# Start of a two-block kernel on one core: the first norm's remainders ahead of its squares, its sums and its spread inside later weight panels, and the layers of the filter network placed later

## The reference, cut to what matters

```python
def rmsnorm(x, g):
    y = x32 * lax.rsqrt(jnp.mean(x32 * x32, axis=-1, keepdims=True) + RMS_EPS)
    return y * g
...
def hyena_filter(L, w1, b1, w2, b2, w3, b3, freq, w_out, decay):
    act = lambda a: jnp.sin(fr * a)
    h = act(feat @ w1 + b1)
    h = act(h @ w2 + b2)
    h = act(h @ w3 + b3)
    h = (h @ w_out).reshape(L, 2, D_MODEL)
    h = h * jnp.exp(-t[:, :, None] * jnp.abs(decay))
...
def hyena_mixer(u, ...):
    z = short_conv(u @ w_in + b_in, conv_w, conv_b)
```

## Time and profile before

| what | value |
|---|---|
| time, median of 3 runs | 2446.01 us (2444.39 to 2450.88) |
| time of the profiled execution | 2445.98 us |
| its span, first to last instruction | 2444.2 us |
| TensorE busy | 97% of the span |
| VectorE, ScalarE, GpSimd busy | 45%, 25%, 27% of the span |
| mean granted clock of TensorE | 0.986 of full speed |

### The profile page before, as it was taken

How to read it: one execution, slowest core, us unless ns; L and a number is a source line. 1 busy time by engine, 2 the same in 40 slices (tenths; PEclk the granted TensorE clock), 3 DMA queues, 4 the chain that set the end, 5 groups by cost and what they waited for, 6 DMA issues and landing times.

```text
span 2444.2 us, 29269 instructions
## 1 busy us (share of the span) xinstructions
PE 2360.0 (97%) x11692; PEld 1899.7 (78%) x11692; DVE 1107.9 (45%) x1131; ACT 604.0 (25%) x672; POOL 657.8 (27%) x378
## 2 busy tenths in 40 slices
PE   7999999799999999999997999999999999999996
PEld 5666773478888888888886888889897877778885
DVE  6765445542662165413366837263543124500533
ACT  4333324422100001002123636262622011111011
POOL 2212211122333333323241121222222233323331
PEclk9999999999999999999998999999999999999998
DMA  4133239512221223112111212020214221112231
GB/s 155 51 122 123 85 134 369 187 43 78 95 86 52 77 80 109 43 43 70 51 61 35 104 36 69 26 77 26 77 34 181 94 78 56 56 43 69 95 121 69
DMA packets 77507, 211.51 MB, mean 87 GB/s; under 512 B 24182, under 2 KB 28088, under 8 KB 77178
## 3 DMA queue, kind: packets, MB, share of 16 engines
q1 hardware_dynamic: 64794, 172.72, 20.7%
q10 hardware_dynamic: 8288, 29.36, 3.1%
q0 software_dynamic: 4352, 8.40, 1.1%
HBM read 165.36 MB, written 40.37 MB: 84 GB/s over the span
## 4 chain that ended last, share of the span: by engine, by line
PE 75%; DVE 3%; ACT 1%; issue 0%; ACTq 0%; DVEq 0%
PE ps L1209 63%; PE ps L539 5%; DVE T L1857 1%; PE ps L1483 1%; PE ps L586 1%; PE ps L605 1%; PE ps L568 1%; PE ps L606 1%; PE ps L607 1%; PE ps L1231 0%; DVE XN L1887 0%; PE ps L1240 0%; DVE X L2181 0%; DVE H L1880 0%; PE ps L505 0%; PE ps L524 0%
## 5 line engine op out<-in xcount | busy, mean ns | idle before, releaser
L1209 PE MATMUL ps<-H,whi 128*128 128x512 f32 x4000 | 1082.3, 392 | 21.9 <-DVE H L1924 11.3
L1209 PEld LDWEIGHTS ps<-H,whi 128*128 128x128 f32 x4000 | 749.9, 188 | 198.5 <-issue 29.6
L1209 PE MATMUL ps<-H,wlo 128*128 128x512 f32 x2000 | 617.7, 390 | 0.0
L1156 POOL CAST whi<-wraw 128x1024 fp32r<-128x1024 f32 x174 | 182.5, 1049 | 1573.0 <-PE ps L1209 844.9
L1158 POOL TENSOR_TENSOR wlo<-wraw,whi 128x1024 fp32r<-128x1024 f32 x178 | 453.6, 2548 | 53.4 <-ACT whi L673 39.5
L1209 PEld LDWEIGHTS ps<-H,wlo 128*128 128x128 f32 x2000 | 376.5, 188 | 79.3
L1209 PE MATMUL ps<-A,whi 128*128 128x512 f32 x1472 | 397.8, 392 | 8.2 <-DVE A L2213 4.9
L1209 PEld LDWEIGHTS ps<-A,whi 128*128 128x128 f32 x1472 | 278.0, 189 | 68.0 <-issue 5.3
L1209 PE MATMUL ps<-A,wlo 128*128 128x512 f32 x736 | 228.1, 391 | 0.0
L1209 PEld LDWEIGHTS ps<-A,wlo 128*128 128x128 f32 x736 | 139.3, 189 | 29.3
L2097 DVE TENSOR_TENSOR T<-ps,T 128x1024 f32<-128x1024 f32 x22 | 26.9, 1224 | 155.7 <-PE ps L1209 155.7
(11 more groups left out here) (337 smaller groups left out, 2310.6 us busy)
## 6 DMA issues: line engine op xcount, KB each, us to landing
wraw<-in_panels SPq DMA_DIRECT2D x181, 512.0 KB, 3.6
mw<-in_modp SPq DMA_DIRECT2D x24, 512.0 KB, 3.5
g<-gsp SPq DMA_DIRECT2D x16, 512.0 KB, 3.7
gr<-g SPq DMA_DIRECT2D x16, 512.0 KB, 9.8
bs<-s SPq DMA_DIRECT2D x16, 512.0 KB, 9.4
YB<-yi POOLq DMA_DIRECT2D x16, 512.0 KB, 8.8
X<-in_xT SPq DMA_DIRECT2D x4, 1024.0 KB, 10.8
s<-sa SPq DMA_DIRECT2D x8, 512.0 KB, 2.7
```

Source lines behind the costliest of these rows:

```text
L1156: nc.gpsimd.tensor_copy(whi[:, s, :, :], wraw[:, s, :, :]).then_inc(hi_made, 1)
L1209: last = mm(p[:, c * step:(c + 1) * step], w[:, ws, k, :], operand(act, a, k, c * step, step), start=(q == 0 and w is whi and a == 0), sto ...
```

## The change

Only orders change, and who splits panel 1. DVE: all eight remainders first, then the remainder of panel 1, then the eight adds. The argument of the filter's first layer is cut in two around them. The arguments of layers 2 and 3 move behind the panel product of zin1 and zin3. ACT: all rounded copies, then the rounding of panel 1, then the squares. PE: zin1 starts ahead of the norm's sums, which come after its sixth k step. The spread comes in the middle of zin2, and mlp1 and mlp2 come one panel later. GpSimd no longer splits panel 1. SyncE issues `vec` ahead of panel 0 and X tiles 0 and 1 apart.

```diff
-PHASES = [("mlp0", 1, 0), ("zin0", 1, 1), ("norm1", 1, 0), ("zin1", 1, 1), ("mlp1", 1, 0), ("zin2", 1, 1),
-          ("mlp2", 1, 0), ("zin3", 1, 1), ("ztap", len(ZTAP), len(ZPANELS)), ...
+PHASES = [("mlp0", 1, 0), ("zin0", 1, 1), ("zin1", 1, 1), ("norm1", 1, 0), ("zin2", 1, 1), ("mlp1", 1, 0),
+          ("zin3", 1, 1), ("mlp2", 1, 0), ("ztap", len(ZTAP), len(ZPANELS)), ...
...
+            sp.dma_start(vec[:, :], d["vec"]).then_inc(vec_in, 16)
             panel(0, 0)
-            sp.dma_start(vec[:, :], d["vec"]).then_inc(vec_in, 16)
-            for k in range(4):
+            for k in range(2):
+                sp.dma_start(X[:, k, :], xv[:, k, :]).then_inc((cx_in, x_in[0])[k], 16)
+            for k in range(1, 4):
                 sp.dma_start(X[:, 2 * k:2 * k + 2, :], xv[:, 2 * k:2 * k + 2, :]).then_inc(x_in[k], 16)
...
+            pool.wait_ge(split_made, 2)
...
             project("zin0", 0, (n1.lo, 0))
             pe.wait_ge(const_in, 16)
+            project("zin1", 0, part=range(KT - 2))
             norm_sums("norm1", (TT[2], n1, KT + 2))
-            project("zin1", 0)
+            project("zin1", 0, part=range(KT - 2, KT))
+            project("zin2", 0, part=range(KT // 2))
             norm_spread("norm1", n1, nr)
+            project("zin2", 0, part=range(KT // 2, KT))
             pe.wait_ge(filt_in, 208)
             mlp("mlp1", 0, fw2, fh, (sin_made, 1))
-            project("zin2", 0)
+            project("zin3", 0)
             mlp("mlp2", 0, fw3, fh, (sin_made, 2))
-            project("zin3", 0)
...
             act.wait_ge(vec_in, 16)
+            A_(nr[:, 0:1], vcol("norm_mix"), ACT.Copy, scale=vcol("norm_mix"))
             for k in range(KT):
...
                 gained_hi(n1, X[:, k, :], H[:, 0, k, :], vcol("norm_mix", k))
+            act.wait_ge(raw_in[1], 16)
+            act.wait_ge(hi_made, 1)
+            A_(whi[:, 1, :, :], wraw[:, 1, :, :], ACT.Copy).then_inc(hi_made, 1)
+            for k in range(KT):
                 square(n1, X[:, k, :], k)
...
-            argument(0)
+            argument_turns(0)
+            for k in range(KT):
+                gained_lo(n1, k, X[:, k, :], H[:, 1, k, :], H[:, 0, k, :], vcol("norm_mix", k))
+            dve.wait_ge(hi_made, 2)
+            dve.wait_ge(split_made, 1)
+            V_.tensor_tensor(wlo[:, 1, :, :], wraw[:, 1, :, :], whi[:, 1, :, :].bitcast(F32), ALU.subtract
+                             ).then_inc(split_made, 1)
+            for k in range(KT):
+                add_square(n1, k, TT[2][:, :], TT[k % 2][:, :])
+            argument_rest(0)
             norm_rstd(n1, "norm1", nv[:, 0:8], nr[:, 0:8], nq[:, 0:8])
...
                 z_tile(ps[s], evac[s], turn(ph, 0) + 1, n, n // 2 + 8 + 8 * (n % 2))
+                if n % 2:
+                    argument_turns(n // 2 + 1)
+                    argument_rest(n // 2 + 1)
                 s_conv(n, n // 2, n % 2)
-                if n < 2:
-                    argument(n + 1)
```

More of the change, by code:

```diff
@@ L1088, in _ @@
             sp.wait_ge(panel_done, N0["up2"])
+            sp.wait_ge(cx_in, 16)
             sp.dma_start(CX[:, :, :], d["ctxT"].rearrange("(k p) t -> p k t", p=P)).then_inc(cx_in, 16)
@@ L1141, in _ @@
         def _(pool):
[L1142 to L1147, removed]
+            pool.wait_ge(raw_in[0], 16)
+            nc.gpsimd.tensor_copy(whi[:, 0, :, :], wraw[:, 0, :, :]).then_inc(hi_made, 1)
+            pool.wait_ge(hi_made, 1)
+            nc.gpsimd.tensor_tensor(wlo[:, 0, :, :], wraw[:, 0, :, :], whi[:, 0, :, :].bitcast(F32), ALU.subtract
+                                    ).then_inc(split_made, 1)
+            pool.wait_ge(split_made, 2)
             def pair(i, quick=False):
@@ L1253, in _, with project @@
             mlp("mlp0", 0, fw1, feat, (feat_in, 32))
-            def project(phase, u, ready=None):
+            def project(phase, u, ready=None, part=range(KT)):
                 n = N0[phase] + u
-                pe.wait_ge(split_made, n + 1)
-                free(phase, u)
-                panel_mm(ps[slot(phase, u)], n % 2, H, T, 8, ready).then_inc(panel_done, 1)
+                if part[0] == 0:
+                    pe.wait_ge(split_made, n + 1)
+                    free(phase, u)
+                last = panel_mm(ps[slot(phase, u)], n % 2, H, T, 8, ready, part=part)
+                if part[-1] == KT - 1:
+                    last.then_inc(panel_done, 1)
             project("zin0", 0, (n1.lo, 0))
             pe.wait_ge(const_in, 16)
+            project("zin1", 0, part=range(KT - 2))
             norm_sums("norm1", (TT[2], n1, KT + 2))
-            project("zin1", 0)
+            project("zin1", 0, part=range(KT - 2, KT))
+            project("zin2", 0, part=range(KT // 2))
             norm_spread("norm1", n1, nr)
+            project("zin2", 0, part=range(KT // 2, KT))
             pe.wait_ge(filt_in, 208)
             mlp("mlp1", 0, fw2, fh, (sin_made, 1))
-            project("zin2", 0)
+            project("zin3", 0)
             mlp("mlp2", 0, fw3, fh, (sin_made, 2))
-            project("zin3", 0)
             def tap_values(m):
@@ L1551, in _ @@
             first_z("zin0", 0, 8)
+            first_z("zin1", 1, 16)
             sine(1)
-            first_z("zin1", 1, 16)
+            first_z("zin2", 2, 9)
+            first_z("zin3", 3, 17)
             act.wait_ge(arg_made, 3)
             A_(hb[:, :, :].rearrange("p a b -> p (a b)"), fu[:, :], ACT.Sin).then_inc(hb_made, 1)
-            first_z("zin2", 2, 9)
-            first_z("zin3", 3, 17)
             def decays(m):
@@ L1713, in _ @@
                 if last:
-                    act.wait_ge(cx_in, 16)
+                    act.wait_ge(cx_in, 32)
                     for k in range(KT):
@@ L1903, in x_tile, with argument_turns @@
                 return X[:, k, :]
-            def argument(l):
+            def argument_turns(l):
                 phase, u = f"mlp{l}", 0
@@ L1928, in _ @@
             dve.wait_ge(vec_in, 16)
-            for k in range(KT):
-                gained_lo(n1, k, X[:, k, :], H[:, 1, k, :], H[:, 0, k, :], vcol("norm_mix", k))
-                add_square(n1, k, TT[2][:, :], TT[k % 2][:, :])
             def v24(name):
```

8 lines of the change are left out of this document (5 added, 3 removed).

## The result

The changed kernel takes 2455.74 us (median of 9 runs, 2453.14 to 2458.2), the kernel before 2447.36 us (median of 9, 2444.39 to 2450.88). The ratio is 1.0036 with a 95% interval from 1.0026 to 1.0046: 8.4 us slower. The interval lies clear of no change, and the difference is just over the 0.3% that the prediction takes as the least it can tell. The profiled execution took 2453.14 us, the lowest of the nine.

A forecast was written before the change was run, and what follows sets the result against it. Bound: TensorE's list from panel 4's first matmul (80.42 us), released by hb at the end of VectorE's chain. hb 5.3 us later plus 2.3 us of clock, +7.6 on 2445.98, gives 2453.6 us; range 2450 to 2456.5, chance 0.80.

The forecast's parts named there:

- More than forecast: Rival: rstd's small operations wait for both GpSimd instructions and R1 slips, or slow matmuls last longer; 2456 to 2460 us, chance 0.06.
- The other two signs: Forecast wrong if R1 ends before 46 us, or if the wait for hb is under 10 us.
- The chain from R1 to hb: VectorE's and ScalarE's filter work from R1's end at 50.4 us until hb lets panel 4 start at 85.7 us.
- the collisions of 0.9 and 0.85 us: In the filter chain: zin1's product behind GpSimd's rounding of panel 4, zin2's convolution behind its subtraction for panel 5.
- The adds' collision: First norm: GpSimd's split of panel 2 falls among VectorE's eight adds and costs 3.2 us, ending them at 37.0 us.
- TensorE's wait at the sums: After six steps of zin1, at 34.6 us, TensorE waits for the adds until 37.1 us.
- The clock at panel 4: Slow matmuls behind some 15 us of TensorE idle time cost 2.3 us, ends 1.4 and 2.6 us.
- TensorE's list decides: Rival: hb is ready when TensorE reaches panel 4, which starts about 10 us earlier; 2436 us, chance 0.04.
- An undisturbed chain: Rival: GpSimd's splits of panels 2, 4 and 5 miss VectorE's operations, 5.0 us fall out; about 2448 us, chance 0.10.
- its cover: rstd's small operations ready at 46.4 us, ahead of the spread, with 0.7 us to spare.

The follow-up runs named there:

- second profile: The changed kernel run once more with no edit, for a second profile: 2457.42 us, ratio 1.0039 to the kernel before.

## Why the prediction was right

The time of 2455.74 us lies 2.1 us over the 2453.6 forecast, inside its own range of 2450 to 2456.5. The mechanism came as forecast: the reordered start ends in a long wait for hb, and the clock is low behind it. That the size fits so well is partly luck. Of the 2.1 us 1.4 are the kernel before itself, whose median is 2447.36 and not 2445.98 us. In the first profiles panel 4 started 1.6 us earlier than forecast and the clock behind it cost 0.5 us less; the later part of the program, which no edit touched, took 1.3 us more, and the medians stand 1.2 us further apart (8.4 us) than the profiled executions (7.2 us). Measured once more, the same kernel came out at 2457.42 us, outside that range and in that of *More than forecast*. The steps, as the forecast gave them and as the changed kernel's first profile has them:

| step | forecast, us | measured, us |
|---|---|---|
| remainders | 11.8 to 22.4 | 12.66 to 22.3 |
| sums start | 37.1 | 36.27 |
| end of R1 | 50.4 | 49.34 |
| argument 2 ends | 65.6 | 64.26 |
| product of zin2 ends | 70.9 | 69.43 |
| argument 3 ends | 84.6 | 82.98 |
| TensorE idle ahead of panel 4 | some 15 | 14.18 |
| panel 4 starts | 85.7 | 84.13 (87.36 in the second profile) |
| clock behind it | 2.3 | 1.76 (2.38) |
| from there to the end | 2363.8 + 2 | 2366.87 (2368.2) |

One of the forecast's own signs of being wrong was met: the time behind panel 4's start was not to change by more than 3 us, and it changed by 3.09 us (2366.87 - 2363.78), 4.5 us in the second profile. Of the 3.09 us 1.76 are the clock right behind the wait. The rest is taken up below. The other two signs were not met.

**The chain from R1 to hb.** Shown. From R1's end to panel 4 the forecast had 35.3 us, the profile has 34.79. The waits for zin1's product (0.88 instead of 0.23 us at its small operation) and for GpSimd's work for panel 5 (an operation of 2.04 instead of 1.28 us) are the collisions of 0.9 and 0.85 us that were put in; they measured 0.65 and 0.76 us. With argument 3 ahead of zin2's convolution the loss shrank by 5.2 us (8.4 to 3.2), as the order says.

**The adds' collision.** The term of 3.2 us measured 2.8 (12.85 less 10.04 us). By itself it was about right; its effect was taken as lateness alone, and for the profiled execution that holds.

**TensorE's wait at the sums.** Mis-sized. The forecast had 2.5 us of idle time (34.6 to 37.1) and no price for the clock there; the profiles have 0 to 1.45 us, and three of seven show a fall of the clock that costs 1.7 to 3.2 us. The price that I gave only to the long wait in front of panel 4 falls due at this short one too.

**The clock at panel 4.** Shown: 1.54 to 2.38 us in the four profiles with a wait of 14.18 us (1.76 and 2.38 us in the two of the changed kernel), and 2.6 us behind the 8.84 us with argument 3 first, all inside 1.4 to 2.6. The Trainium skill (TensorE: Matmul & The Clock Gate, Part 1: The HAM clock gate) says that the number of slow matmuls varies with the run. The traces agree: in the two profiles of the changed kernel 12 and 6 matmuls were clearly slow at the start of zin0.

**The rest.** The first matmul of the transform after the filter comes at 272.38 us before and 277.68 after, and from there to the end the two take 2171.8 and 2173.3 us. In eleven other profiles of kernels that have the same code there it was 2171.4 to 2177.5 us. So the 1.5 us lie inside the spread of this later part, and nothing ties them to the change.

**The rivals.** *TensorE's list decides* did not come about, for the reason given: the chain after R1 got longer. But that chain stood in the way only through one wait that panel 4 doesn't need, and that I took as given. With the wait moved, the 10 us of that rival still don't come: 2.7 us, and 8.1 us with less work on VectorE, which bounds next. *An undisturbed chain* was tested by holding GpSimd: 5.4 instead of 8.4 us over before. That is one collision of the three, 2.8 us. The rival's own sum gave it too much: without it the adds end at 33.8 us, but TensorE comes to the sums at 34.6, so 2.5 and not 3.2 us could fall out there, and 4.3 instead of 5.0 us in all. *More than forecast* is what the second set of runs shows, but at the sums and not at rstd, which kept its cover (45.38 us for 46.34).

**What stays open.** The medians (8.4 and 10.8 us over before in two sets of runs) exceed the 6.8 us between the two first profiles. The fall at the sums explains 1 us in the mean. The first profile is also of the fastest of its nine executions. What the rest is stays open: it may be slow matmuls in later parts, but no run tried which.

## What to carry to other kernels

An engine that comes earlier to a wait has won nothing until what it waits for comes earlier too: before moving work forward, follow each wait behind it to the end of the list that feeds it, and ask whether the instruction behind the wait needs it at all. Here the reordering alone lost 8 us, and the same reordering with the wait put at its first reader, and with GpSimd kept away from the adds, was 5 us faster than before. Whether the reordering is worth its trouble beside the late wait alone isn't shown: the old order with it was 1.9 us under before. When a wait of 14 us is removed, look at once for the next engine that is nearly full, and for what of its time is waiting for another engine.

## What the runs showed of the hardware

- A short wait can cost more than its length. At the sums 1.06 to 1.45 us of idle time and the sums themselves (16 matmuls 128x1, some 2 us) were followed by slow matmuls for 4 to 6 us, with a granted clock of 0.50 to 0.60 from 38 to 42 us, and a loss of 1.7 to 3.2 us. With waits of 0 to 0.41 us there the clock was 1.00. Yet 1.50 to 1.6 us of idle time ahead of panel 4 (before, and with TensorE kept at work) or of zin3 were followed by warm matmuls. The length of the wait alone doesn't decide it. No run separates the part of the wait from that of the small matmuls of the sums, which stand only there.
- The first matmuls of zin0 in the same kernel were slow for 12 in one execution and for 6 in another, and the execution with fewer ended 4.6 us later (a span of 2455.6 against 2451.0 us). 3.2 of them stand at panel 4 already, and follow from TensorE's early arrival at the next wait.
- An operation between SBUF tiles on VectorE and one on GpSimd excluded each other, also where one is tiny: 128x8 took 2.17 instead of 0.17 us behind a subtraction of GpSimd of 2.40 us. So these engines do not meet only at semaphores, as the text ahead of the prediction has it. The Trainium skill (GPSIMD Engine Reference, section 8, Key points) says that GpSimd shares its SBUF interfaces with VectorE, with contention for VectorE's instructions in a 2-port mode or with two SBUF inputs. The rows for two SBUF inputs agree and give it a size: up to nearly the whole of the other engine's instruction. An operation with one SBUF input was held too: fu took 2.05 instead of 0.69 us (at 9.85 us, beside GpSimd's subtraction until 11.34 us); which mode it runs in, no row shows.
